# Conformer layer norm: variance sums laid out over token partitions, the inverse root spread back by TensorE

## Chip, cores and metric

One core of one Trainium2 chip runs the program once. The metric is the device time of that core in microseconds (us); lower is better. TensorE (PE) does matrix products, VectorE (DVE), ScalarE (ACT) and GpSimd (POOL) the rest, and SyncE (SP) issues the weight loads.

## The reference, cut to what matters

Two blocks run over a stream of 512 tokens by 1024 features. The change lies in the second block's second layer, in the convolution module and its layer norm:

```
def layernorm(x, g, b):
    mu = jnp.mean(x32, axis=-1, keepdims=True)
    var = jnp.mean(jnp.square(x32 - mu), axis=-1, keepdims=True)
    return ((x32 - mu) * lax.rsqrt(var + LN_EPS) * g + b).astype(x.dtype)

def conformer_conv(h, w_in, b_in, dw, dw_b, ln_g, ln_b, w_out, b_out):
    u = h @ w_in + b_in
    u = u[..., :D] * jax.nn.sigmoid(u[..., D:])
    u = causal_dwconv(u, dw) + dw_b
    u = jax.nn.silu(layernorm(u, ln_g, ln_b))
    return u @ w_out + b_out
```

After it comes a cross attention, whose keys and values `memn @ w_kv` depend on the memory alone and so can be computed at any time before.

## The kernel before

Everything is kept transposed: features on the 128 partitions, in KD = 8 tiles `m`, and the 512 tokens along the free dimension. A product runs as a `Linear` stage. One output tile of it is 8 x 3 matmuls (a float32 weight is split into a rounded part `w_hi` and a rest `w_lo`, and so is the input, L363 to L365), its weights are one chunk of 128 x 1024, and the split of each chunk is done two chunks ahead: ACT makes `w_hi` (L452), POOL `w_lo` (L460). Each engine's instructions stand in the order in which the Python methods of the stages write them; nothing is reordered, and every hand-over is a semaphore.

The three stages here are: the convolution's input product; `kv`, the 16 tiles of keys and values with 256 columns (`ms_hi`, `ms_lo`, outputs in PSUM banks 4 to 7); and `out`, the product with `w_out`, whose input tiles `ys_hi` and `ys_lo` are the normed, activated convolution. The layer norm has no stage of its own. It is written into the steps `t` = 0 to 15 of `kv`: `memory_tensor` is called after tile `t`'s matmuls on PE, and `memory_scalar` at the same step on ACT, behind the split of a chunk and behind `keys.taken`, which copies tile `t` out of PSUM (L2640) and so waits for its matmuls. `memory_vector` is one piece of DVE work.

The steps of the norm, with the names of the program: the mean by products with a matrix of ones (L2927); `gn_centred`, the mean taken off `conv_y` by DVE (L2955); `gn_squared`, the squares `ln_sq` by ACT (L2981, step 12); `gn_var`, the sum of the squares over features (`variance_tensor`, L2935); `gn_root` (L2984); `gn_inverse` (L2957); then for each `m` the product with gain and inverse root on DVE (L2965, `gn_scaled`), Silu on ACT (L2988), the rounded `ys_hi` on ACT (L2990) and the rest `ys_lo` on DVE (L2962, `fed`). PE's first tile of `out` takes the pairs `ys_hi`, `ys_lo` one `m` at a time as `fed` reports them, and every later tile of `out` follows without a wait.

Of the kernel before, what the change touches and what calls it, by code (L numbers as in the profile page):

```python
# [8 lines left out]
ACT = mybir.ActivationFunctionType  # L9
# [3 lines left out]
P = 128  # L13
T = 512
D = 1024
KD = D // P
# [51 lines left out]
class Signal:  # L68


    def __init__(self, nc, name):
        self.sem = nc.alloc_semaphore(name)
        self.base = 0
# [95 lines left out]
def as_float(t):  # L169

    return t.bitcast(F32)
# [1392 lines left out]
class Recurrence:  # L1564
# [184 lines left out]
    def spread_tensor(self, pe, p):  # L1749

        if p:
            self.wait(pe, "key_normed", p)
        else:
            self.wait(pe, "kk_inverse", 2)
        self.done(pe.matmul(self.k.ps[:, 6, :], self.spread[0:2 * KD, self.chunk(p)], self.rt[0:2 * KD, :], start=True,
                            stop=True), "spread")
# [1051 lines left out]
class Conformer:  # L2808
# [5 lines left out]
    def __init__(self, k, at, top, ready, prev):  # L2814
        self.k = k
        room = at(17)
        self.u, self.sg = at(0).tile("conv_u", KD, T + TAPS - 1), room.tile("conv_s", 2, T)
        self.rt, self.y, self.diag = room.tile("ln_rt", T), at(64).tile("conv_y", KD, T), at(80).tile("conv_dg", 4, PE_TAPS, P)
        self.sq = Arena(k, top).tile("ln_sq", KD, T)
        self.out = Halves(at(0).tile("ys_hi", KD, T, dtype=F32R), at(80).tile("ys_lo", KD, T, dtype=F32R))  # L2820
        self.used, self.free, self.sig_r, self.scaled = k.marks("chunk_used", "bank_free", "sigmoid_made", "normed_sums")
        self.dg, self.padz, self.summed, self.added, self.kept = k.marks("diagonals", "zeroed", "taps_summed", "taps_added",
                                                                         "conv_taken")
        self.norm = k.marks("gn_mean", "gn_centred", "gn_squared", "gn_var", "gn_root", "gn_inverse", "gn_scaled",
                            "gn_shifted", "fed_hi", "fed")
        self.handed = self.norm[9]
        self.linear = Linear(k, 2 * KD, KD, k.ahead, act=self.inputs_scalar, vector=self.inputs_vector, pool=self.inputs_pool,
                             fill=self.inputs_tensor, unroll=True, norm=True, bank=4, ready=ready, prev=prev)
        k.advance(KD, "sigmoid_made", "taps_summed", "conv_taken")
        k.advance(2 * KD, "normed_sums")  # L2830
        k.advance(KD * PE_TAPS, "diagonals")
        k.advance(1, "zeroed", "gn_mean", "gn_var", "gn_root", "gn_inverse")
        k.advance(KD * (TAPS - PE_TAPS), "taps_added")
        k.advance(KD, "gn_centred", "gn_squared", "gn_scaled", "gn_shifted", "fed_hi", "fed")
# [95 lines left out]

    def variance_tensor(self, pe, m):

        sq = self.norm[2]
        pe.wait_ge(sq.sem, sq(m + 1))
        mm = pe.matmul(self.k.ps[:, 1, :], self.k.ones[:, :], self.sq[:, m, :], start=(m == 0), stop=(m == KD - 1))  # L2935
        if m == KD - 1:
            mm.then_inc(self.norm[3].sem, 1)

    def memory_tensor(self, pe, t):
        if t == 0:  # L2940
            self.taps_tensor(pe, KD - 1)
        for m in {6: (0, 1, 2), 7: (3, 4, 5), 11: (6, 7)}.get(t, ()):
            self.mean_tensor(pe, m)
        for m in {13: (0, 1, 2, 3), 14: (4, 5, 6, 7)}.get(t, ()):
            self.variance_tensor(pe, m)

    def memory_vector(self, v, i, j):
        if i or j:
            return
        k, y = self.k, self.y  # L2950
        me, ce, sq, va, rt, iv, n1, n2, hi, fed = self.norm
        self.taps_vector(v, self.BOUNDS[KD], 4 * self.PAIR_OPS)
        v.wait_ge(me.sem, me(1))
        for m in range(KD):
            v.scalar_tensor_tensor(y[:, m, :], k.ps[:, 0, :], -1.0 / D, y[:, m, :], ALU.mult, ALU.add).then_inc(ce.sem, 1)  # L2955
        v.wait_ge(rt.sem, rt(1))
        v.reciprocal(k.ps[:, 2, :], self.rt[:, :]).then_inc(iv.sem, 1)  # L2957
        v.wait_ge(iv.sem, iv(1))

        def rest(m):  # L2960
            v.wait_ge(hi.sem, hi(m + 1))
            v.tensor_tensor(self.out.lo[:, m, :], y[:, m, :], as_float(self.out.hi[:, m, :]), ALU.subtract  # L2962
                            ).then_inc(fed.sem, 1)
        for m in range(KD):
            v.scalar_tensor_tensor(y[:, m, :], y[:, m, :], k.vec("cln_g", m), k.ps[:, 2, :], ALU.mult, ALU.mult  # L2965
                                   ).then_inc(n1.sem, 1)
            if m >= 2:
                rest(m - 2)
        rest(KD - 2)
        rest(KD - 1)  # L2970

    def memory_scalar(self, act, i, j):
        k, y, m = self.k, self.y, 4 * i + j
        me, ce, sq, va, rt, iv, n1, n2, hi, fed = self.norm
        self.keys.taken(act, 4, m)
        if m in (4, 10):
            self.keep(act, {4: 2, 10: 3}[m])
        if m == 12:
            for n in range(KD):
                act.wait_ge(ce.sem, ce(n + 1))  # L2980
                act.activation(self.sq[:, n, :], y[:, n, :], ACT.Square).then_inc(sq.sem, 1)  # L2981
        if m == 14:
            act.wait_ge(va.sem, va(1))
            act.activation(self.rt[:, :], k.ps[:, 1, :], ACT.Sqrt, scale=1.0 / D, bias=k.bias[1e-5]).then_inc(rt.sem, 1)  # L2984
        if m == 15:
            for n in range(KD):
                act.wait_ge(n1.sem, n1(n + 1))
                act.activation(y[:, n, :], y[:, n, :], ACT.Silu, bias=k.vec("cln_b", n)).then_inc(n2.sem, 1)  # L2988
                act.wait_ge(n2.sem, n2(n + 1))
                act.activation(self.out.hi[:, n, :], y[:, n, :], ACT.Copy).then_inc(hi.sem, 1)  # L2990


def conv_ffn(k, layer, at, tmp, ready, gain=None):
# [300 lines left out]
```

## Time and profile before

| | us |
|---|---|
| Time, median of 3 runs | 2587.29 (2586.89 to 2590.23) |
| The profiled execution: its time | 2576.17 |
| The profiled execution: its span | 2574.4 |
| PE busy over the span | 2484.3 |

The span runs from the first to the last instruction of the profile; 1.8 us of the profiled execution's time lie around it. The profiled execution was 11 us shorter than the median of the timed runs, so a change is worked out against its own time and then added to the median.

### The profile page before, as it was taken

What the parts mean: (1) busy time and instruction counts of PE and PEld (TensorE: products, weight loads), DVE (VectorE), ACT (ScalarE), POOL (GpSimd) and SP (SyncE); (2) the same over time, 40 slices, a digit from 0 to 9 for tenths busy, and PEclk for the clock granted to TensorE, in tenths of its full rate; (3) what the DMA queues carried; (4) which work ended last, traced back from release to release, by engine and by line L of the source; (5) the groups of instructions that cost most, each with busy time, mean ns of one, the idle gap of its engine ahead of it and who ended that gap; (6) DMA issues with size and microseconds to landing.
All of it is one profiled execution on the core that took longest, in us unless ns stands there. A gap on an engine that the chain in (4) does not pass through costs nothing.

```text
span 2574.4 us, 32184 instructions
## 1 busy us (share of the span) xinstructions
PE 2484.3 (96%) x12188; PEld 1927.1 (75%) x12188; DVE 1163.2 (45%) x1969; ACT 937.1 (36%) x1580; POOL 1021.0 (40%) x618
## 2 busy tenths in 40 slices
PE   7999999999989999999999999999999899999997
PEld 5776567888846668885787888888767787888886
DVE  5113744113052675734623364264399433562462
ACT  3544653222245462223433323123323534322222
POOL 4331545444522332212552544345324443444344
PEclk9999999999999999999999999999999999999998
DMA  3222012333311110002331233223222222233231
GB/s 123 65 66 87 18 34 90 99 97 93 124 49 52 56 58 2 2 1 93 116 106 46 92 94 112 77 94 100 80 66 90 91 82 66 86 95 114 82 98 66
DMA packets 54415, 196.98 MB, mean 77 GB/s; under 512 B 6573, under 2 KB 6701, under 8 KB 53581
## 3 DMA queue, kind: packets, MB, share of 16 engines
q1 hardware_dynamic: 53312, 192.44, 23.8%
q10 hardware_dynamic: 974, 2.80, 0.3%
q8 instruction: 84, 1.38, 0.2%
q14 instruction: 45, 0.37, 0.1%
HBM read 193.12 MB, written 2.10 MB: 76 GB/s over the span
## 4 chain that ended last, share of the span: by engine, by line
PE 45%; DVE 7%; ACT 1%; issue 0%; POOLq 0%; POOL 0%; DVEq 0%; ACTq 0%
PE ps L363 11%; PE ps L365 11%; PE ps L364 11%; DVE ps L2878 5%; PE ps L436 3%; PE ps L438 3%; PE ps L437 3%; PE ps L2721 1%; PE ps L2744 1%; PE ps L2891 1%; DVE ps L3040 0%; PE ps L2489 0%; PE ps L2521 0%; PE ps L2731 0%; PE ps L2935 0%
## 5 line engine op out<-in xcount | busy, mean ns | idle before, releaser
L460 POOL TENSOR_TENSOR w_lo<-raw,w_hi 128x1024 fp32r<-128x1024 f32 x342 | 819.3, 2406 | 1008.9 <-ACT w_hi L452 1008.8
L363 PE MATMUL ps<-ahead_hi,w_hi 128*128 128x512 f32 x1216 | 481.0, 396 | 2.0 <-issue 2.0
L365 PE MATMUL ps<-ahead_hi,w_lo 128*128 128x512 f32 x1216 | 473.3, 389 | 0.0
L364 PE MATMUL ps<-ahead_lo,w_hi 128*128 128x512 f32 x1216 | 473.1, 389 | 0.0
L452 ACT ACTIVATE w_hi<-raw 128x1024 fp32r<-128x1024 f32 x342 | 352.9, 1049 | 170.4 <-PE ps L438 91.1
L621 DVE TENSOR_TENSOR x_stream<-x_stream,ps 128x512 f32<-128x512 f32 x80 | 55.0, 687 | 474.5 <-PE ps L365 278.5
L363 PEld LDWEIGHTS ps<-ahead_hi,w_hi 128*128 128x128 f32 x1216 | 228.3, 188 | 52.9 <-issue 6.4
L364 PEld LDWEIGHTS ps<-ahead_lo,w_hi 128*128 128x128 f32 x1216 | 228.3, 188 | 50.9 <-issue 4.1
L365 PEld LDWEIGHTS ps<-ahead_hi,w_lo 128*128 128x128 f32 x1216 | 228.2, 188 | 48.0
L3012 ACT ACTIVATE ffn_s<-ps 128x512 f32<-128x512 f32 x44 | 26.3, 598 | 322.2 <-DVE ps L3040 322.2
L436 PE MATMUL ps<-ffn_a_hi,w_hi 128*128 128x512 f32 x352 | 137.4, 390 | 3.0 <-DVE ffn_a_lo L3045 2.9
L438 PE MATMUL ps<-ffn_a_hi,w_lo 128*128 128x512 f32 x352 | 137.0, 389 | 0.0
L437 PE MATMUL ps<-ffn_a_lo,w_hi 128*128 128x512 f32 x352 | 136.9, 389 | 0.0
L2878 DVE SCALAR_TENSOR_TENSOR ps<-conv_u,vecs,ps 128x512 f32<-128x512 f32 x192 | 127.1, 748 | 14.5 <-PE ps L2891 14.5
L654 POOL TENSOR_TENSOR squares<-squares,sqr 128x512 f32<-128x512 f32 x56 | 74.7, 1333 | 126.5 <-ACT sqr L645 70.8
L3023 DVE TENSOR_TENSOR ffn_u<-ps,root 128x512 f32<-128x512 f32 x88 | 60.6, 688 | 133.1 <-PE ps L365 133.0
L3040 DVE SCALAR_TENSOR_TENSOR ps<-ffn_u,vecs,ps 128x512 f32<-128x512 f32 x176 | 119.8, 749 | 0.0
L363 PE MATMUL ps<-hidden_hi,w_hi 128*128 128x512 f32 x256 | 99.6, 389 | 0.0
L364 PE MATMUL ps<-hidden_lo,w_hi 128*128 128x512 f32 x256 | 99.6, 389 | 0.0
L365 PE MATMUL ps<-hidden_hi,w_lo 128*128 128x512 f32 x256 | 99.6, 389 | 0.0
L363 PE MATMUL ps<-h_hi,w_hi 128*128 128x512 f32 x192 | 79.7, 415 | 17.1 <-DVE w_lo L245 13.3
L644 ACT ACTIVATE ahead_hi<-x_stream,vecs 128x512 fp32r<-128x512 f32 x48 | 34.8, 725 | 142.6 <-DVE x_stream L621 115.4
(419 smaller groups left out, 4579.4 us busy)
## 6 DMA issues: line engine op xcount, KB each, us to landing
raw<-in_wall SPq DMA_DIRECT2D x346, 512.0 KB, 3.6
x_stream<-in_x SPq DMA_DIRECT2D x8, 256.0 KB, 7.2
cw<-in_cmp_w SPq DMA_DIRECT2D x1, 2048.0 KB, 8.0
out_y<-x_stream SPq DMA_DIRECT2D x8, 256.0 KB, 2.1
lora_a<-in_lora_a ACTq DMA_DIRECT2D x1, 1152.0 KB
dist<-in_consts SPq DMA_DIRECT2D x1, 1088.0 KB, 11.1
mem<-in_mem SPq DMA_DIRECT2D x1, 1024.0 KB, 5.7
gwb<-in_lora_b SPq DMA_DIRECT2D x1, 1024.0 KB
```

Source lines behind the costliest of these rows:

```text
L363: pe.matmul(out, hi, src.hi[:, t, 0:width], start=first, stop=False)
L364: pe.matmul(out, hi, src.lo[:, t, 0:width], start=False, stop=False)
L365: return pe.matmul(out, lo, src.hi[:, t, 0:width], start=False, stop=last)
L436: pe.matmul(out, hi, src.hi[:, q, 0:width], start=(q == 0), stop=False)
L437: pe.matmul(out, hi, src.lo[:, q, 0:width], start=False, stop=False)
L438: mm = pe.matmul(out, lo, src.hi[:, q, 0:width], start=False, stop=(q == kt - 1))
L452: e.activation(self.w.hi[:, s, :], self.raw[:, s, :], ACT.Copy).then_inc(hi_r.sem, 1)
L460: e.tensor_tensor(self.w.lo[:, s, :], self.raw[:, s, :], as_float(self.w.hi[:, s, :]), ALU.subtract).then_inc(lo_r.sem, 1)
L654: e.tensor_tensor(k.squares[:, :], k.squares[:, :], sqt[:, m % 2, :], ALU.add).then_inc(ac.sem, 1)
L2878: v.scalar_tensor_tensor(bank, self.u[:, m, t:t + T], self.tap(m, t), bank, ALU.mult, ALU.add).then_inc(self.added.sem, 1)
L3023: e.tensor_tensor(ub[:, j, 2:T + 2], k.ps[:, 4 + j, :], k.root[:, :], ALU.mult).then_inc(ub_r.sem, 1)
L3040: e.scalar_tensor_tensor(bank, ub[:, m % 4, t:t + T], col, bank, ALU.mult, ALU.add).then_inc(cv.sem, 1)
```

## The change

The sum of squares over features is computed the other way round. Before, the 128 x 128 ones were the stationary operand and the squares of all 512 tokens the moving one, four feature tiles after `kv` tile 13 and four after tile 14; the sum of every token came out on all 128 partitions. Now the squares are the stationary operand, in four blocks of 128 tokens, and one column of ones moves: 32 matmuls whose output is one column each, all after tile 13. A token's sum then stands on one partition, and the sums fill a 128 x 4 tile. ACT takes the root of 128 x 4 numbers in step 13 instead of 128 x 512 in step 14; DVE inverts 128 x 4. `spread_tensor`, new, follows `kv` tile 14 on PE: four matmuls with the inverse roots of a block, broadcast along the free dimension, as stationary operand and the identity as moving one, which lay the inverse root of every token on all partitions of PSUM bank 2. DVE's scaling waits for this (`gn_spread`). On ACT, Silu and rounding of the first two feature tiles move from step 15 to step 14, ahead of a split and of the copy of tile 15.

```diff
     def variance_tensor(self, pe, m):
-        sq = self.norm[2]
+        ce, sq = self.norm[1:3]
+        if m == 0:
+            pe.wait_ge(ce.sem, ce(KD))
         pe.wait_ge(sq.sem, sq(m + 1))
-        mm = pe.matmul(self.k.ps[:, 1, :], self.k.ones[:, :], self.sq[:, m, :], start=(m == 0), stop=(m == KD - 1))
+        for b in range(4):
+            mm = pe.matmul(self.k.ps[:, b, 0:1], self.sq[:, m, b * P:(b + 1) * P], self.k.ones[:, 0:1], start=(m == 0),
+                           stop=(m == KD - 1))
         if m == KD - 1:
             mm.then_inc(self.norm[3].sem, 1)
+    def spread_tensor(self, pe):
+        iv = self.norm[5]
+        pe.wait_ge(iv.sem, iv(1))
+        for b in range(4):
+            mm = pe.matmul(self.k.ps[:, 2, b * P:(b + 1) * P], self.rt[:, 8 + b:9 + b].to_broadcast([P, P]), self.k.ident, start=True,
+                           stop=True)
+        mm.then_inc(self.spread.sem, 1)
     def memory_tensor(self, pe, t):
-        for m in {13: (0, 1, 2, 3), 14: (4, 5, 6, 7)}.get(t, ()):
-            self.variance_tensor(pe, m)
+        if t == 13:
+            for m in range(KD):
+                self.variance_tensor(pe, m)
+        if t == 14:
+            self.spread_tensor(pe)
     def memory_vector(self, v, i, j):
-        v.reciprocal(k.ps[:, 2, :], self.rt[:, :]).then_inc(iv.sem, 1)
-        v.wait_ge(iv.sem, iv(1))
+        v.reciprocal(self.rt[:, 8:12], self.rt[:, 0:4]).then_inc(iv.sem, 1)
+        v.wait_ge(self.spread.sem, self.spread(1))
     def memory_scalar(self, act, i, j):
-        if m == 14:
+        if m == 13:
             act.wait_ge(va.sem, va(1))
-            act.activation(self.rt[:, :], k.ps[:, 1, :], ACT.Sqrt, scale=1.0 / D, bias=k.bias[1e-5]).then_inc(rt.sem, 1)
-        if m == 15:
-            for n in range(KD):
+            act.activation(self.rt[:, 0:4], k.ps[:, 0:4, 0], ACT.Sqrt, scale=1.0 / D, bias=k.bias[1e-5]).then_inc(rt.sem, 1)
+        for n in {14: (0, 1), 15: range(2, KD)}.get(m, ()):
```

On PE, this is the place from the end of `kv` tile 13 to the end of tile 14, before the change (`ps<-ln_sq,ones` are the sums of squares, the other rows the matmuls of `kv`):

```order
L2935 MATMUL ps<-ln_sq_10656,ones 128x512 x4
L363 MATMUL ps<-ms_hi_10627,w_hi_10622 128x256
L364 MATMUL ps<-ms_lo_10628,w_hi_10622 128x256
L365 MATMUL ps<-ms_hi_10627,w_lo_10623 128x256
...
L2935 MATMUL ps<-ln_sq_10656,ones 128x512 x4
```

And the same place of the changed kernel:

```order
L2940 MATMUL ps<-ones,ln_sq_10656 128x1 x32
L363 MATMUL ps<-ms_hi_10627,w_hi_10622 128x256
L364 MATMUL ps<-ms_lo_10628,w_hi_10622 128x256
L365 MATMUL ps<-ms_hi_10627,w_lo_10623 128x256
...
L2950 MATMUL ps<-consts,ln_rt_10653 128x128 x4
```

All squares are summed ahead of tile 14 now, in 32 matmuls of one output column, and where the second half of the sums stood there are the four matmuls of the spread.

On ACT, this is the place from the squares (step 12) to the first rounded tiles (step 15), before the change (`ln_rt` is the root, `conv_y` the Silu in place, `kv_turned` the copy of a `kv` tile):

```order
L2981 ACTIVATE ln_sq_10656<-conv_y_10654 128x512 x8
L452 ACTIVATE w_hi_10622<-raw_10621 128x1024
L2640 ACTIVATE kv_turned_10631<-ps 128x256
L452 ACTIVATE w_hi_10622<-raw_10621 128x1024
L2640 ACTIVATE kv_turned_10631<-ps 128x256
L2984 ACT_TABLE_LOAD
L2984 ACTIVATE ln_rt_10653<-ps,eps 128x512
L452 ACTIVATE w_hi_10622<-raw_10621 128x1024
L2640 ACTIVATE kv_turned_10631<-ps 128x256
L2988 ACT_TABLE_LOAD
L2988 ACTIVATE conv_y_10654<-conv_y_10654,vecs 128x512
L2990 ACTIVATE ys_hi_10657<-conv_y_10654 128x512
```

And in the changed kernel, from the copy of tile 13 to the third Silu:

```order
L3002 ACT_TABLE_LOAD
L3002 ACTIVATE ln_rt_10653<-ps,eps 128x4
L452 ACTIVATE w_hi_10622<-raw_10621 128x1024
L2640 ACTIVATE kv_turned_10631<-ps 128x256
L3005 ACT_TABLE_LOAD
L3005 ACTIVATE conv_y_10654<-conv_y_10654,vecs 128x512
L3007 ACTIVATE ys_hi_10657<-conv_y_10654 128x512
L3005 ACTIVATE conv_y_10654<-conv_y_10654,vecs 128x512
L3007 ACTIVATE ys_hi_10657<-conv_y_10654 128x512
L452 ACTIVATE w_hi_10622<-raw_10621 128x1024
L2640 ACTIVATE kv_turned_10631<-ps 128x256
L3005 ACTIVATE conv_y_10654<-conv_y_10654,vecs 128x512
```

The root stands one split and one copy earlier, and two Silus with their roundings stand ahead of the last split and the last copy, which now lie between the second and the third Silu.

## Rows read from the trace of the kernel before

**Rows 1.** The page, part 1: busy us (share of the span), instructions

```profile
PE 2484.3 (96%) x12188; PEld 1927.1 (75%) x12188; DVE 1163.2 (45%) x1969; ACT 937.1 (36%) x1580; POOL 1021.0 (40%) x618
```

**Rows 2.** The chain that ended last, 1960 to 2060 us: start, us, what

```profile
2009.79 3.43 PE ps L2935 x8
...
2019.56 0.70 ACT ln_rt L2984
2020.29 3.37 DVE ps L2957
...
2035.56 0.50 PE ps L363
2036.06 0.23 PE ps L364
```

**Rows 3.** PE's timeline: start, us, engine, line, operation, idle before it and releaser

```profile
2009.63 3.59 PE L2935 MATMUL ps<-ln_sq,ones 128*128 128x512 f32 x8
2012.66 0.68 PE L363 MATMUL ps<-ms_hi,w_hi 128*128 128x256 f32 x1
...
2015.93 3.59 PE L2935 MATMUL ps<-ln_sq,ones 128*128 128x512 f32 x8
...
2026.72 0.77 PE L363 MATMUL ps<-ys_hi,w_hi 128*128 128x512 f32 x1 [4.33 <-DVE ys_lo L2962]
```

**Rows 4.** ACT's timeline, 2007 to 2028 us

```profile
2007.23 4.26 ACT L2981 ACTIVATE ln_sq<-conv_y 128x512 f32<-128x512 f32 x8
2011.39 1.04 ACT L452 ACTIVATE w_hi<-raw 128x1024 fp32r<-128x1024 f32 x1
2012.34 0.36 ACT L2640 ACTIVATE kv_turned<-ps 128x256 f32<-128x256 f32 x1
...
2016.13 0.38 ACT L2640 ACTIVATE kv_turned<-ps 128x256 f32<-128x256 f32 x1 [2.48 <-PE ps L365]
2016.53 1.28 ACT L2984 ACT_TABLE_LOAD   x1
...
2022.43 0.38 ACT L2640 ACTIVATE kv_turned<-ps 128x256 f32<-128x256 f32 x1 [1.23 <-PE ps L365]
2022.83 1.28 ACT L2988 ACT_TABLE_LOAD   x1
2024.46 0.72 ACT L2988 ACTIVATE conv_y<-conv_y,vecs 128x512 f32<-128x512 f32 x1 [0.35 <-DVE conv_y L2965]
...
2027.03 0.71 ACT L2988 ACTIVATE conv_y<-conv_y,vecs 128x512 f32<-128x512 f32 x1
```

**Rows 5.** PE's timeline, 39 to 42 us, in the first block's gates

```profile
39.66 1.85 PE L813 MATMUL ps<-gates_w,xg 128*128 128x12 f32 x16
41.37 0.48 PE L363 MATMUL ps<-h_hi,w_hi 128*128 128x512 f32 x1
```

**Rows 6.** DVE's timeline, 2001 to 2024 us

```profile
2004.09 4.88 DVE L2955 SCALAR_TENSOR_TENSOR conv_y<-ps,conv_y 128x512 f32<-128x512 f32 x8 [2.80 <-PE ps L2927]
```

**Rows 7.** Groups by line and shape: line, operation, shapes, count | busy, mean ns | idle before

```profile
L2756 DVE RECIPROCAL xst<-xst 128x1 f32<-128x1 f32 x32 | 5.1, 160 | 2.6 <-ACT xp L2773 2.1
```

**Rows 8.** PE's timeline: the same sixteen L2136 matmuls twice, and an L2106 group

```profile
999.49 3.68 PE L2136 MATMUL ps<-X,Tt 128*128 128x64 f32 x16
...
1028.80 2.00 PE L2136 MATMUL ps<-X,Tt 128*128 128x64 f32 x16
...
1105.36 1.14 PE L2106 MATMUL ps<-Tt,U 64*64 64x64 f32 x16
```

**Rows 9.** Windows: length, busy of PE, PEld, DVE, ACT, POOL, granted clock, DMA share, GB/s

```profile
998.00:1006.00 8.00, 8.00 (x52) 7.22 (x49) 0.46 (x2) 1.14 (x4) 2.48 (x5) 0.50 0.00 0
...
1106.50:1107.00 0.50, 0.50 (x3) 0.50 (x4) 0.00 (x0) 0.46 (x1) 0.00 (x0) 0.66 0.00 0
1107.00:1110.00 3.00, 3.00 (x22) 2.44 (x21) 0.00 (x0) 0.28 (x2) 0.00 (x0) 0.50 0.00 0
1110.00:1110.50 0.50, 0.50 (x6) 0.50 (x6) 0.00 (x0) 0.50 (x3) 0.00 (x0) 0.93 0.00 0
...
2024.50:2025.00 0.50, 0.00 (x0) 0.00 (x0) 0.50 (x1) 0.50 (x1) 0.00 (x0) 0.84 0.56 90
...
2031.50:2032.00 0.50, 0.50 (x3) 0.27 (x2) 0.50 (x2) 0.47 (x2) 0.00 (x0) 0.83 0.00 0
```

More of the change, by code:

```diff
@@ L2825, in __init__ @@
                             "gn_shifted", "fed_hi", "fed")
+        self.spread = k.marks("gn_spread")
+        k.advance(1, "gn_spread")
         self.handed = self.norm[9]
@@ L2981, in memory_scalar @@
                 act.activation(self.sq[:, n, :], y[:, n, :], ACT.Square).then_inc(sq.sem, 1)
-        if m == 14:
+        if m == 13:
             act.wait_ge(va.sem, va(1))
-            act.activation(self.rt[:, :], k.ps[:, 1, :], ACT.Sqrt, scale=1.0 / D, bias=k.bias[1e-5]).then_inc(rt.sem, 1)
-        if m == 15:
-            for n in range(KD):
[L2987 to L2990, printed above, removed]
+            act.activation(self.rt[:, 0:4], k.ps[:, 0:4, 0], ACT.Sqrt, scale=1.0 / D, bias=k.bias[1e-5]).then_inc(rt.sem, 1)
+        for n in {14: (0, 1), 15: range(2, KD)}.get(m, ()):
+            act.wait_ge(n1.sem, n1(n + 1))
+            act.activation(y[:, n, :], y[:, n, :], ACT.Silu, bias=k.vec("cln_b", n)).then_inc(n2.sem, 1)
+            act.wait_ge(n2.sem, n2(n + 1))
+            act.activation(self.out.hi[:, n, :], y[:, n, :], ACT.Copy).then_inc(hi.sem, 1)
 def conv_ffn(k, layer, at, tmp, ready, gain=None):
```

## Prediction

> **What bounds the kernel now.** I began with the page's busy times: PE is busy 2484.3 us, 96% of the span [rows 1], so only work that PE does, or a wait of PE, is worth time. Next I read the chain that ended last around the norm. Nearly everywhere it is PE; here it leaves PE. It goes through the last four of the variance matmuls, then the root on ACT (0.70 us), then the inverse on DVE (3.37 us), and comes back to PE at 2035.56 us with the last input tile of `out` [rows 2]. PE's timeline shows the hole: tile 15 of `kv` follows the second half of the sums, and then PE sits idle 4.33 us, until `ys_lo` releases it at 2026.72 [rows 3]. ACT's timeline shows what sets the pace from there. The first Silu starts at 2024.46, the third at 2027.03, so one feature tile takes 1.28 us (Silu and rounding together) [rows 4]. The eighth reaches PE at 2035.56 [rows 2], 8.53 us after the third Silu. PE needs less than that for a feature tile's three matmuls. From 2035.56 on PE runs without a wait. So the time of the kernel moves by exactly as much as this last feature tile moves, and that one hangs on the start of the Silus.
>
> **The change, term by term.** All starts come from rows; what runs before 2009.63 is untouched.
>
> *The sums on PE.* Removed: two groups of four matmuls, each 8 records in 3.43 us [rows 2], together 6.86 us. Added: 32 matmuls with 128 x 128 float32 weights and one moving column. A float32 matmul shows as two records, so 64. The nearest row is the gates' product: the same weights, 12 moving columns. Its 16 records take from 39.66 to 41.37, 0.107 us each [rows 5]; it is paced by the weight loads, which do not shrink with the columns. 64 x 0.107 = 6.84 us. The lower bound is a record that hides its weight load (priced as a rival); the upper is the clock, below. I take 0.107. So PE's total work is the same to 0.02 us, and only its place changes: all 6.84 us stand ahead of tile 14, none behind it. Sums end at 2009.63 + 6.84 = 2016.47. The wait for the squares costs nothing: eight squares take 4.26 us from 2007.23 [rows 4], 0.53 each, and PE takes 0.86 for each. The new wait for `gn_centred` is over when DVE's last subtraction ends, 2004.09 + 4.88 = 2008.97 [rows 6], 0.66 us before PE gets there.
>
> *Root and inverse.* Before, the root started about 0.2 us behind the last sum. Now it starts at about 2016.65 and has 4 numbers per partition instead of 512. The table load of 1.28 us is no obstacle: it can start behind the copy of tile 13 at 2012.34 [rows 4] and is over by 2014.2. The inverse of 128 x 512 took 3.37 us [rows 2]; the nearest small one takes 0.160 us [rows 7]. Both are over by 2017.1, while PE is in tile 14, so the 3.37 us leave the path.
>
> *The spread.* Tile 14 took from 2012.66 to 2015.93 [rows 3]; it moves by 6.84 - 3.43 = 3.41 us and ends at 2019.34. The four spread matmuls are 8 records at 0.107 (bounded by 0.125, the sixteen records in 2.00 us of [rows 8]): 0.86 to 1.0 us. With 0.2 us of hand-over DVE starts scaling at 2020.4 and the first Silu could start 0.78 later, at 2021.2.
>
> *ACT.* Its copy of tile 14 moves from 2016.13 [rows 4] to 2019.54. The Silu table load followed the copy by 0.40 us and took 1.28 [rows 4]: 2019.94 to 2021.22. So both paths meet and the first Silu starts at 2021.25 instead of 2024.46, 3.2 us earlier. But between the second and the third Silu there are now a split and the copy of tile 15, 0.95 + 0.26 = 1.21 us, by the distances of the same two instructions at 2011.39 and 2012.34 [rows 4]. Waiting behind them are Silus 3 to 8, and for those PE. Tile 15 has ended by then (2020.2 + 3.3 = 2023.5 against 2024.8), so this is no further wait. Third Silu: 2021.25 + 2.57 + 1.21 = 2025.03 against 2027.03. **Sum at full clock: -2.0 us.** The split delayed by this (chunk for `out` tile 1, needed by PE at about 2036) and the one delayed by the root in step 13 (chunk for tile 0) are POOL's next; both are made by 2027 (by 2031 with the fall below), before they are needed, and the weight loads of SP that hang on them have four chunks of lead.
>
> *The clock.* The sum above has a condition: for 6.84 us PE multiplies almost nothing, one column per weight load. The profile shows that the clock can fall although PE never stands still. At 1105.36 to 1106.43 PE runs 64-column matmuls [rows 8] and at 1106.66 (0.66 in the half microsecond from 1106.50) the granted clock goes to 0.50, the 1.2 GHz level, with PE busy in every row [rows 9]. From 998 to 1006 it stays there for the whole eight microseconds under 64- and 128-column matmuls [rows 9], and the sixteen L2136 records take 3.68 us in it instead of 2.00 [rows 8]. These matmuls carry 64 columns or more; ours carry one. So I expect the clock to fall inside the sums and to come back inside tile 14 or after it. All of the PE work in such a stretch is on the path (sums, tile 14, spread), and at half clock a stretch costs half its length. The stretches of this profile: 1106.66 to 1110.03, 3.4 us; 2024.84 to 2031.59 (worked out like the first from the rows with 0.84 and 0.83), about 6.8; and over 8 from 998 on, about 10 [rows 9]. Costs: 1.7, 3.4 and about 5. I take the middle one, since the low-activity work here goes on for some time after the fall, as there. Cost 3.4. Everything behind the sums moves with it, the Silu table load too. **Sum with the fall: -2.0 + 3.4 = +1.4 us**, between -0.3 and +3.0.
>
> The Trainium skill, "TensorE: Matmul & The Clock Gate", in the table under "Why this matters for your kernels", ties a falling clock to gaps in which TensorE is idle and advises issuing matmuls back to back. There is no gap here, so by that rule the change would give -2.0 us. The rows at 1106 speak against it: the clock fell with no gap.
>
> The Trainium skill, "ScalarE: Activation LUTs", section "What ACT_TABLE_LOAD costs", adds a drain of about 1.38 us to each load of 1.28 us. By that the first Silu would wait until about 2022.6 and the full-clock sum be -0.7 us. The load at 2022.83 had its Silu running 0.35 us after its end, and that gap was a wait for DVE, so the trace does not show the drain behind a load.
>
> **The rivals.** (1) *The clock stays up* (the page's rule as a mechanism): weight loads count as activity, or the sums end before the clock reacts. For it speaks that the gates' 12-column burst ran at full pace; but it lasted only 1.85 us [rows 5]. -2.0 us, 2585.3. Chance 0.13. (2) *A slower kernel*: the clock is still at half when the last feature tile enters PE. Up to then ACT's pace hides it, since three 512-column matmuls at half clock take about the 1.28 us that ACT takes. Behind it, nothing hides it, and each of the 24 matmuls of an `out` tile takes 0.46 instead of 0.23 us [rows 2], 5.5 us more per tile. With one whole tile that is 1.4 + 5.5 = +6.9, 2594.2. It decides from about 17 slow matmuls on (3.8 us lost). For it: the two gaps of PE behind the second feature tile, now some 1.8 us because of the split and copy. Against: a rise at about 2031.6 under just such fed-in matmuls [rows 9]. Chance 0.04. (3) *Weight loads hidden*: if one-column records cost a third, 2.3 us in all, tile 14 starts at about 2012 and the Sqrt table load (done 2014.2) and the copy set the Silus, first Silu about 2017.3; -7.2 + 1.2 = -6.0, 2581.3. [rows 5] speak clearly against it. Chance 0.03. The likeliest, the fall, has 0.80.
>
> **How the numbers follow.** Own time: 2576.17 + 1.4 = 2577.6 for a profiled execution; the median is 2587.29, which gives 2588.7. The three timed runs spread by 3.3 us, so I widen the cases' 2585.3 to 2590.3 by about 1.5 on each side: 2584 to 2592. A change of 0.2% is 5.2 us, about what a measurement of this kernel can tell from no change; both likely cases are well within it, whichever sign. Within: 0.90. Faster by more: rival 3 and a lucky clock, 0.05. Slower by more: rival 2, 0.05.
>
> **What would show it.** The 64 records at 0.107 us each in the beginning and 0.21 after a fall; granted clock 0.5 from some point between 2012 and 2016.5 until inside or just behind tile 14; inverse below 0.2 us; first Silu near 2021.3 without a fall and near 2024.6 with it; 3.8 us from the first to the third Silu instead of 2.57; last feature tile on PE at 2033.6 without and near 2037 with the fall. Wrong would be: a start-to-start well under 0.107, a full clock throughout, or a low clock in `out` tile 1.

## The result and the profile after

| | before | after |
|---|---|---|
| Median, 12 runs each, us | 2587.8 (2581.25 to 2591.73) | 2594.0 (2580.01 to 2595.68) |
| Ratio after to before | | 1.0018, 95% interval 1.0009 to 1.0026 |
| Span of the profiled execution, us | 2574.4 | 2593.4 |

By the ratio the change costs about 4.7 us, 0.18%, with an interval of 2.3 to 6.7 us; the two medians lie 6.2 us apart. The ratio's value is the forecast direction at more than three times the forecast size of 1.4 us, and the median lies above the range of 2584 to 2592. The two first profiles differ by 19 us, most of which has nothing to do with the change: the first sum of squares starts at 2009.63 us before [rows 3] and at 2023.72 after, so 14 us were there already (the last section comes back to it). The measure used from here on is therefore a *local time*: from PE's first sum to the start of the last input tile in `out` tile 0. Before it is 2035.56 - 2009.63 = 25.93 us [rows 2, 3].

PE's timeline of the changed kernel, with the rows that answer to [rows 3] and the last input tile:

```profile
2023.72 11.68 PE L2940 MATMUL ps<-ones,ln_sq 128*128 128x1 f32 x64
2035.26 0.56 PE L363 MATMUL ps<-ms_hi,w_hi 128*128 128x256 f32 x1
...
2040.09 1.05 PE L2950 MATMUL ps<-consts,ln_rt 128*128 128x128 f32 x8
...
2044.24 0.47 PE L363 MATMUL ps<-ys_hi,w_hi 128*128 128x512 f32 x1 [0.23 <-DVE ys_lo L2980]
2045.43 0.50 PE L363 MATMUL ps<-ys_hi,w_hi 128*128 128x512 f32 x1 [0.26 <-DVE ys_lo L2980]
2048.64 0.50 PE L363 MATMUL ps<-ys_hi,w_hi 128*128 128x512 f32 x1 [2.25 <-DVE ys_lo L2980]
...
2054.30 0.50 PE L363 MATMUL ps<-ys_hi,w_hi 128*128 128x512 f32 x1
```

The local time is 2054.30 - 2023.72 = 30.58 us, 4.65 us more than before. The 64 records of the sums take 11.54 us up to the start of tile 14, instead of 6.84. The old hole of 4.33 us is gone, and a new one of 2.25 us stands behind the second feature tile, where ACT makes a split and a copy.

Windows of the same execution (length, busy of the five engines, granted clock, DMA share, GB/s):

```profile
2023.70:2025.70 2.00, 2.00 (x21) 2.00 (x19) 0.00 (x0) 2.00 (x5) 0.00 (x0) 1.00 0.78 254
2026.00:2039.00 13.00, 13.00 (x62) 13.00 (x62) 0.18 (x1) 3.29 (x5) 4.63 (x2) 0.50 0.14 42
2039.50:2044.00 4.50, 4.50 (x38) 4.31 (x37) 2.66 (x4) 3.63 (x5) 0.00 (x0) 1.00 0.34 117
```

PE counts as busy in every microsecond, yet the granted clock is 0.50, the 1.2 GHz level, from 2.2 us behind the first sum until just before the spread. (Row by row in half microseconds the stretch adds up to 13.65 us.) Each of the thirteen profiles below has one more low stretch, in the first tile of `out`: 2024.84 to 2031.67 before, 2049.8 to 2053.2 in the changed kernel. It costs nothing there: from the start of the third Silu to the last input tile it is 8.53 to 8.55 us in all of them, so ACT's pace hides it.

ACT's and DVE's timelines show that the rest of the change does what it should:

```profile
2035.43 0.26 ACT L3002 ACTIVATE ln_rt<-ps,eps 128x4 f32<-128x4 f32 x1 [7.34 <-PE ps L2940]
...
2040.29 0.38 ACT L2640 ACTIVATE kv_turned<-ps 128x256 f32<-128x256 f32 x1 [3.65 <-PE ps L365]
2040.69 1.28 ACT L3005 ACT_TABLE_LOAD   x1
2041.98 0.72 ACT L3005 ACTIVATE conv_y<-conv_y,vecs 128x512 f32<-128x512 f32 x1
...
2045.77 0.71 ACT L3005 ACTIVATE conv_y<-conv_y,vecs 128x512 f32<-128x512 f32 x1
```

```profile
2035.73 0.18 DVE L2975 RECIPROCAL ln_rt<-ln_rt 128x4 f32<-128x4 f32 x1 [12.68 <-ACT ln_rt L3002]
```

The inverse takes 0.18 us instead of the 3.37 us of [rows 2]. The first Silu starts straight behind its table load; from it to the third Silu there are 3.79 us instead of the 2.57 us of [rows 4].

### The profile page after: what moved, and what is told of

Same layout as the page of the kernel before. It is cut to its first block, busy times and chain, and to the rows that moved or that the text cites. A ratio compares the mean times of both kernels' runs of the same rounds, so it can differ in the third digit from the quotient of the medians.

```text
span 2593.4 us, 32297 instructions
## 1 busy us (share of the span) xinstructions
PE 2507.9 (97%) x12244; PEld 1950.6 (75%) x12244; DVE 1160.8 (45%) x1969; ACT 936.9 (36%) x1580; POOL 1020.9 (39%) x618
## 4 chain that ended last, share of the span: by engine, by line
PE 46%; DVE 6%; ACT 1%; issue 0%; POOLq 0%; POOL 0%; DVEq 0%; ACTq 0%
PE ps L363 11%; PE ps L365 11%; PE ps L364 11%; DVE ps L2880 4%; PE ps L436 3%; PE ps L437 3%; PE ps L438 3%; PE ps L2721 1%; PE ps L2744 1%; PE ps L2893 1%; PE ps L2940 0%; DVE ps L3057 0%; PE ps L2489 0%; PE ps L2521 0%; PE ps L2731 0%
## 5 line engine op out<-in xcount | busy, mean ns | idle before, releaser
L363 PE MATMUL ps<-ahead_hi,w_hi 128*128 128x512 f32 x1216 | 482.0, 396 | 2.0 <-issue 2.0
L363 PEld LDWEIGHTS ps<-ahead_hi,w_hi 128*128 128x128 f32 x1216 | 228.7, 188 | 53.2 <-issue 6.4
L363 PE MATMUL ps<-hidden_hi,w_hi 128*128 128x512 f32 x256 | 99.6, 389 | 0.0
L363 PE MATMUL ps<-h_hi,w_hi 128*128 128x512 f32 x192 | 79.6, 414 | 17.2 <-DVE w_lo L245 13.7
```

Of the source, the lines that this page charges most:

```text
L363: pe.matmul(out, hi, src.hi[:, t, 0:width], start=first, stop=False)
```

## Experiments

**The theories.** Theory 1: the whole loss is TensorE's clock. One-column matmuls occupy PE but give it next to nothing to multiply; the clock goes to its lower level inside the sums, and that low stretch lies on the path. Without it the change would gain about 2 us. Rival: the clock is a side show, and the loss comes from the order of ACT (split and copy between the Silus) or from 32 small matmuls and their hand-overs.

All local times, worked out from the same two rows of each profile. wide, wide15, order15, halves and twice are edits of the changed kernel; whole13, early and early2 are edits of the kernel before; after_b and before_b are the two kernels unedited. after_b, before_b, twice, wide15, halves and halves_b were executed once each, so only their local times are used:

| kernel | first sum | last input tile | local us | clock in sums and `kv` tiles |
|---|---|---|---|---|
| before | 2009.63 | 2035.56 | 25.93 | 1.00 |
| before_b | 2022.72 | 2048.65 | 25.93 | 1.00 |
| after | 2023.72 | 2054.30 | 30.58 | 0.50 for 13.65 us |
| after_b | 2022.73 | 2053.33 | 30.60 | 0.50 for 13.65 us |
| wide | 2022.09 | 2046.31 | 24.22 | 1.00 |
| wide15 | 2013.41 | 2040.17 | 26.76 | 1.00 |
| order15 | 2021.87 | 2051.80 | 29.93 | 0.50 for 6.83 us |
| halves | 2009.89 | 2038.79 | 28.90 | 0.50 twice, 6.83 us together |
| halves_b | 2024.05 | 2056.07 | 32.02 | 0.50 twice, 13.66 us together |
| twice | 2021.31 | 2065.55 | 44.24 | 0.50 from 2 us on |
| whole13 | 2008.59 | 2032.86 | 24.27 | 1.00 |
| early | 2024.27 | 2048.21 | 23.94 | 1.00 |
| early2 | 2024.00 | 2047.33 | 23.33 | 1.00 |

**wide: more columns behind the same weight loads.**

```diff
-            mm = pe.matmul(self.k.ps[:, b, 0:1], self.sq[:, m, b * P:(b + 1) * P], self.k.ones[:, 0:1], start=(m == 0),
+            mm = pe.matmul(self.k.ps[:, b, 0:P], self.sq[:, m, b * P:(b + 1) * P], self.k.ones[:, :], start=(m == 0),
```

> One edit of the changed kernel: 128 columns of ones move past each block of squares instead of one, so the same 32 weight loads and products issue in the same order, and only PE's arithmetic per load is larger. Local measure: from the first sum matmul to the last input tile of out on PE, 25.9 us before (2009.63 to 2035.56), 30.6 us after the change (2023.72 to 2054.30). Theory 1 (the clock fell because one-column matmuls are next to no work, and all of the loss is the low stretch over the sums and tile 14): the granted clock stays 1.00 through sums and tile 14, the sums take 64 x 0.107 to 0.125 = 6.8 to 8.0 us instead of 11.5, local 23.9 to 25.0, time about 2 us under before. Rival (the loss is the order of ACT, or the loads and hand-overs of 32 small matmuls): local stays near 30.6 and the time near that of the changed kernel.

PE's timeline and windows of wide:

```profile
2022.09 7.31 PE L2940 MATMUL ps<-ones,ln_sq 128*128 128x128 f32 x64
2029.16 0.36 PE L363 MATMUL ps<-ms_hi,w_hi 128*128 128x256 f32 x1
...
2032.10 1.05 PE L2950 MATMUL ps<-consts,ln_rt 128*128 128x128 f32 x8
...
2046.31 0.50 PE L363 MATMUL ps<-ys_hi,w_hi 128*128 128x512 f32 x1
```

```profile
2022.09:2029.10 7.01, 7.01 (x65) 7.01 (x64) 0.00 (x0) 4.36 (x7) 2.35 (x1) 1.00 0.29 91
2029.10:2037.00 7.90, 7.67 (x62) 7.20 (x60) 3.82 (x7) 5.82 (x9) 2.39 (x1) 1.00 0.37 119
```

128 times the columns, and the sums take less time: 64 records in 7.07 us, 0.110 each, against 11.54 us. The clock stays at 1.00. Local 24.22 us, 6.4 us under the changed kernel and 1.7 under before. Theory 1 holds, and the rival is out as the cause of the loss: the order of ACT, the number of matmuls and their hand-overs are the same in these two kernels. The time was 2586.99 us, the ratio to before 0.9974 (0.9957 to 0.9991); 0.26% is 6.7 us, more than the 1.7 us that the local time accounts for. The likely reason is told in the last section: five of its eleven runs lay at 2572 to 2577 us, with a mean granted clock of 0.987 to 0.989 against 0.981 in the others. Its median is only 0.9 us below that of the kernel before (2587.89 us). So the whole time fits a gain but does not measure it; the 1.7 us rest on the local time.

**after_b and before_b: the two kernels once more.**

> The changed kernel once more, for a second look at where the clock falls. Theory 1: it falls inside the sums again, 2 to 6 us behind the first, and stays down into tile 14; local is 24.2 us (what wide measured at full clock) plus half of the low stretch, so 27.5 to 31. Rival (the fall in the first profile was chance): clock 1.00 there and local 24.2.

> The kernel before once more: clock 1.00 from the first sum to the end of tile 15 and local 25.9 us, whatever the time of the whole kernel does.

Both local times repeat to 0.02 us. Here the first sum starts at the same time in both (2022.73 and 2022.72), and the spans of 2592.4 and 2586.8 us differ by much less than the first pair: 5.6 us, of which 4.7 are local and 0.9 lie behind the last input tile.

**twice: the dose doubled.** The accumulation over feature tiles is left out, so its root is of other numbers.

```diff
-        for b in range(4):
+        for b in (0, 1, 2, 3, 0, 1, 2, 3):
             mm = pe.matmul(self.k.ps[:, b, 0:1], self.sq[:, m, b * P:(b + 1) * P], self.k.ones[:, 0:1], ...
```

> The changed kernel with each of the 32 one-column matmuls issued twice, so 128 records instead of 64 (accumulation over feature tiles is left out, each sum holds the last tile only). Theory 1: the clock falls early in them and cannot come back before they end, so the 64 more cost 0.213 us each: 13.6 us more, local 41 to 45 us, low stretch above 20 us. Rival (a low stretch has its length whatever runs in it, the clock then returns): the added ones cost 0.107 each, local about 6.8 us above the changed kernel's.

PE's timeline and a window of twice:

```profile
2021.31 25.26 PE L2940 MATMUL ps<-ones,ln_sq 128*128 128x1 f32 x128
...
2065.55 0.47 PE L363 MATMUL ps<-ys_hi,w_hi 128*128 128x512 f32 x1
```

```profile
2024.00:2046.00 22.00, 22.00 (x104) 22.00 (x105) 0.00 (x0) 1.67 (x3) 2.35 (x1) 0.50 0.07 25
```

Local 44.24 us, 13.7 more than the changed kernel; 64 x 0.213 = 13.6. Once down, the clock did not come back while these matmuls went on. It is one profile, but far from the 6.8 us that a low stretch of fixed length would have added.

**halves: the one-column sums back in two places.**

```diff
-        if t == 13:
-            for m in range(KD):
-                self.variance_tensor(pe, m)
-        if t == 14:
+        for m in {13: (0, 1, 2, 3), 14: (4, 5, 6, 7)}.get(t, ()):
+            self.variance_tensor(pe, m)
+        if t == 15:
             self.spread_tensor(pe)
```

Not shown: the root moves to step 14 and all Silus to step 15.

> The one-column sums in the places of the old ones, four feature tiles behind tile 13 and four behind tile 14, root in step 14, spread behind tile 15, all Silus in step 15. Theory 1 in the form that a full 6.8 us of one-column work in one piece is what brings the clock down: two pieces of 3.4 us with a tile of 2.9 us between may leave it at 1.00; then sums 3.4 us each, first Silu 14.5 us behind the first sum, local about 25.6. If each piece alone is enough, the clock is at 0.50 in one of them or in a tile, and local is 27 to 29.

> The same kernel as halves again, since where the clock moves differs from run to run: 25.6 with the clock at 1.00, 27 to 29 with a fall.

PE's first piece in halves and the tile behind it, then windows in that tile and in the one behind the second piece:

```profile
2009.89 3.63 PE L2940 MATMUL ps<-ones,ln_sq 128*128 128x1 f32 x32
2013.38 0.36 PE L363 MATMUL ps<-ms_hi,w_hi 128*128 128x256 f32 x1
```

```profile
2015.50:2018.00 2.50, 2.50 (x15) 2.50 (x13) 0.00 (x0) 0.31 (x1) 1.99 (x1) 0.50 0.58 182
2022.50:2024.50 2.00, 2.00 (x11) 2.00 (x11) 0.00 (x0) 0.23 (x1) 1.69 (x1) 0.50 0.00 0
```

And in halves_b, from inside each piece into the tile behind it:

```profile
2027.00:2032.00 5.00, 5.00 (x24) 5.00 (x25) 0.00 (x0) 1.06 (x2) 4.62 (x2) 0.50 0.31 84
2037.00:2043.00 6.00, 6.00 (x29) 6.00 (x30) 0.18 (x1) 1.21 (x2) 2.38 (x1) 0.50 0.05 8
```

My hope that a tile of 2.9 us between two pieces would hold the clock was wrong in both profiles. The clock fell once for each piece of 16 matmuls: in halves_b inside the pieces (at 2026.2 and 2036.5), in halves only behind them, in the full-size matmuls of the next tile (at 2014.6 and 2021.7). 25.6 us were expected without a fall; 28.90 and 32.02 came. The second lies above my 27 to 29 as well: again I took the stretches too short.

**order15 and wide15: the reordering on ACT.** order15 is the changed kernel with this edit, wide15 is wide with it.

```diff
-        for n in {14: (0, 1), 15: range(2, KD)}.get(m, ()):
+        for n in {15: range(KD)}.get(m, ()):
```

> The changed kernel with all eight Silus in step 15, behind the copy of tile 15. With the sums as slow as in the changed kernel's profile: the Silu table load waits for tile 15, first Silu some 3.9 us later, but no split and copy between second and third (1.2 us), so local 30.6 + 2.6 = 33.2 us. Rival (the order of ACT causes the loss): local falls to 26 to 29.

> wide (128 columns moving, clock kept) with all eight Silus in step 15, to price the reordering on ACT at full clock. Tile 15 ends about 3.9 us behind tile 14, so the copy, the Silu table load and the first Silu come 3.9 us less about 0.1 later than in wide, and no split and copy (1.2 us) stand between second and third: local 24.2 + 2.6 = 26.8 us. If the reordering is worth nothing, 24.2.

PE's timelines, first of order15, then of wide15:

```profile
2021.87 9.04 PE L2940 MATMUL ps<-ones,ln_sq 128*128 128x1 f32 x64
2030.78 0.56 PE L363 MATMUL ps<-ms_hi,w_hi 128*128 128x256 f32 x1
...
2051.80 0.50 PE L363 MATMUL ps<-ys_hi,w_hi 128*128 128x512 f32 x1 [0.31 <-DVE ys_lo L2980]
```

```profile
2013.41 7.31 PE L2940 MATMUL ps<-ones,ln_sq 128*128 128x128 f32 x64
...
2040.17 0.50 PE L363 MATMUL ps<-ys_hi,w_hi 128*128 128x512 f32 x1 [0.31 <-DVE ys_lo L2980]
```

wide15 settles it at full clock: 26.76 us, 2.54 above wide, where 2.6 was worked out. So two Silus in step 14 gain 2.5 us. And 26.76 is 0.83 above the kernel before: without them the earlier sums and the small inverse gain nothing. In the kernel before the Silu table load ends at 2022.83 + 1.28 = 2024.11, only 0.35 us ahead of the first Silu [rows 4], so the inverse held the first Silu back by no more than that as long as all Silus stood in step 15. order15 came out at 29.93, not 33.2, because my expectation took the low stretch of the first profile as given; here the clock fell only 5.1 us behind the first sum, the sums took 8.91 us instead of 11.54, and the stretch was 6.83 us. By its own clock it fits: wide15's 26.76 plus half of 6.83 is 30.2. Its time was 2595.23 us, ratio 1.0024 (1.0011 to 1.0038). It also shows that the low stretch over the same sums can differ in length: here it was 6.83 us, in both profiles of the changed kernel 13.65. What sets the moment of the fall, 2.2 us behind the first sum in after, after_b, twice and halves_b and about 5 in order15 and halves, stays open.

**whole13, early, early2: is the small inverse needed?** All three are edits of the kernel before. whole13 takes before's sums (ones stationary, 512 columns moving) and its wide inverse, and only moves them: all sums behind tile 13, root in step 13, two Silus in step 14, no spread.

```diff
-        for m in {13: (0, 1, 2, 3), 14: (4, 5, 6, 7)}.get(t, ()):
-            self.variance_tensor(pe, m)
+        if t == 13:
+            for m in range(KD):
+                self.variance_tensor(pe, m)
-        if m == 14:
+        if m == 13:
             act.wait_ge(va.sem, va(1))
-        if m == 15:
-            for n in range(KD):
+        for n in {14: (0, 1), 15: range(2, KD)}.get(m, ()):
```

> The sums as before the change (ones stationary, 512 columns moving), but all eight behind tile 13; root of 128 x 512 in step 13, the inverse of 128 x 512 on DVE as before, no spread; two Silus in step 14 as in the change. Theory 1: clock stays 1.00 in sums and tile 14, sums 6.86 us, root 0.7, inverse 3.4 us now beside tiles 14 and 15, first Silu 12.0 us behind the first sum, plus 3.8 to the third, local 24.2 us, that is 1.7 under before: the move of the sums gives the gain, and the small inverse and the spread add 0.3 us at most. Rival (the gain needs the 0.2 us inverse): local 25.9 or more.

DVE's timeline and ACT's first Silu in whole13:

```profile
2016.38 3.36 DVE L2958 RECIPROCAL ps<-ln_rt 128x512 f32<-128x512 f32 x1 [8.46 <-ACT ln_rt L2985]
```

```profile
2018.92 1.28 ACT L2988 ACT_TABLE_LOAD   x1
2020.55 0.72 ACT L2988 ACTIVATE conv_y<-conv_y,vecs 128x512 f32<-128x512 f32 x1 [0.34 <-DVE conv_y L2966]
```

The wide inverse costs 0.34 us of waiting here, as it runs beside the `kv` tiles and the table load. Local 24.27 us against wide's 24.22, which has the small inverse and the spread: the new layout is worth 0.05 us once the sums are moved. The time, 2588.14 us, ratio 0.9998 (0.999 to 1.0007), cannot show 1.7 us. early and early2 then make the last chunk's split ahead of the first Silu. early calls it in step 14 behind the copy of tile 14; early2 makes it in the `Linear` stage, ahead of that copy. The edit of early2:

```diff
                 if not (peel and ...) and (i, j) != getattr(self, "early", None):
                     self.split_step(i, j, step)
+                if (i, j + 1) == getattr(self, "early", None):
+                    self.split_step(i, j + 1, step)
...
+        self.kv.early = (3, 3)
```

> As whole13, and the split of the last chunk, which stood between the second and the third Silu, is made in step 14 ahead of the first Silu, where ACT waits for tile 14. Theory 1 with the ACT term of the sum: the distance from first to third Silu falls from 3.8 to 2.9 us, local 23.3 us, 2.6 under before. Rival (the split is not on the path): local as whole13.

> As early, with the last chunk's split made in front of the copy of tile 14, where ACT really waits (in early it stood behind that copy and pushed the first Silu from 11.96 to 12.58 us behind the first sum). Expected: first Silu at 12.0, third at 14.8, local 23.3 us against 25.93 before and 24.27 in whole13. If the split of a chunk cannot be made there without a wait, local as in early, 23.9.

In early, behind the copy, ACT was no longer idle, and the split pushed the first Silu back from 11.96 to 12.58 us behind the first sum: 23.94 us, not 23.3. ACT's timeline of early2:

```profile
2031.65 2.00 ACT L452 ACTIVATE w_hi<-raw 128x1024 fp32r<-128x1024 f32 x2
2033.93 0.38 ACT L2642 ACTIVATE kv_turned<-ps 128x256 f32<-128x256 f32 x1 [0.29 <-PE ps L365]
2034.34 1.28 ACT L2992 ACT_TABLE_LOAD   x1
2035.97 0.72 ACT L2992 ACTIVATE conv_y<-conv_y,vecs 128x512 f32<-128x512 f32 x1 [0.35 <-DVE conv_y L2970]
```

Both splits fit before the copy, the first Silu is 11.97 us behind the first sum (2024.00), and local is 23.33 us, 2.6 under before, the shortest here. Times: early 2587.15 us, ratio 1.0001 (0.999 to 1.0012); early2 2587.38 us, ratio 0.9994 (0.9985 to 1.0003). That early2 beats the kernel before is shown in the local time of one profile, not in the time of the whole.

## Why the prediction was wrong

- **What bounds the place**: right. The time moved with the last input tile: 4.65 us in the local time, 4.7 by the ratio. That they agree so closely is partly chance, as the ratio's interval is 2.3 to 6.7 us.
- **Sums at full clock, 0.107 us a record, 6.84 us**: not seen in the changed kernel; the nearest is wide, 7.07 us with 128 columns. In halves the first piece ran at full clock throughout, 32 records in 3.49 us up to the next tile, 0.109 each, so the term holds for one column as long as the clock does.
- **Root, inverse, spread**: right (0.26 and 0.18 us, spread 0.81 us up to tile 15 with the clock back up). The spread never had to wait for the inverse.
- **ACT**: right. Table load straight into the first Silu, 3.79 us to the third against 3.78 worked out. The drain that the Trainium skill adds to a table load ("ScalarE: Activation LUTs", "What ACT_TABLE_LOAD costs") does not show in this trace: the load starts 0.02 us after the copy ends, and the first Silu 0.01 us after the load ends.
- **Sum at full clock, -2.0 us**: wide gave -1.71, with sums of 7.07 us instead of 6.84.
- **That the clock falls, though PE never stands still**: right, and the rule of the Trainium skill that was weighed against it ("TensorE: Matmul & The Clock Gate", "Why this matters for your kernels", which names idle gaps) would have given -2.0 us. In these traces the clock fell in stretches without a gap.
- **The step that failed**: "I take the middle one", a low stretch of 6.8 us for 3.4 us of cost. It was 13.65 us. The excess over wide is 6.36 us instead of 3.4: 4.47 in the sums (11.54 against 7.07) and 1.89 in tile 14 (4.83 against 2.94). With wide's -1.71 that makes the +4.65. I had listed stretches of 3.4, 6.8 and 10 us as the bounds and thought the longest, 3.0 us in total, the worst. But those lengths came from other work, and this work lengthens itself: once the clock is down, the rest of the sums takes twice as long. In the eight stretches of after, after_b, order15, twice, halves and halves_b the clock came back 3.0 to 5.6 us behind the last one-column matmul before it, whether the whole stretch was 3.4 or 27.3 us long. Had the clock fallen 2.1 us into the sums, they alone were 2.1 + 44 x 0.213 = 11.5 us, which the rows at hand would have given; a range that reached to such an early fall would have held the result.
- **Where luck came in**: 6.8 us was not impossible. order15 has the same sums and a stretch of 6.83 us, and lies 3.2 us above wide15, close to the 3.4 of the forecast. The forecast direction, slower, hung on the same number: with wide's -1.71 us, a low stretch shorter than about 3.4 us would by my estimate have left a gain.
- **Two smaller errors that changed nothing**: the granted clock of 0.93 and 0.83 in the last half microseconds [rows 9] puts the ends of the two shorter stretches at 1110.07 and 2031.67, not 1110.03 and 2031.59; their lengths stay 3.4 and 6.8 us. The two gaps of PE behind the second feature tile, taken as 1.8 us, measured 2.25 and 0.30.

## To carry to other kernels

In these traces a record of a product with 128 x 128 float32 weights took 0.107 to 0.110 us at full clock whether 1, 12 or 128 columns moved. A run of such products with one column also lost the clock, for itself and for the full-size matmuls behind it; with 128 columns it did not. Where more columns cost no time, move many. When the fall of a clock is a term of the sum, price the case in which it falls at the start and the low-work run goes on at half speed, not a stretch length seen elsewhere. And before a new layout is built to shorten an operation, look whether moving the old one a step earlier already hides it: here that, with the two Silus, gave 1.66 of the 1.71 us, and wide15 shows that the two Silus were what it hung on.

## What the runs showed of the hardware

The two profiles of the same kernel, before and before_b, took 2576.17 and 2588.5 us with the same local time. Windows of the first, then of before_b, in the second block's first layer and behind it:

```profile
1150.00:1180.00 30.00, 29.70 (x280) 25.51 (x279) 11.54 (x36) 9.24 (x22) 5.02 (x8) 1.00 0.01 2
1195.00:1215.00 20.00, 17.98 (x48) 4.59 (x47) 5.83 (x9) 11.26 (x20) 7.92 (x9) 1.00 0.63 245
```

```profile
1155.00:1180.00 25.00, 25.00 (x183) 21.34 (x182) 5.19 (x15) 6.71 (x15) 4.92 (x8) 0.73 0.01 2
1195.00:1220.00 25.00, 21.96 (x102) 10.80 (x100) 7.57 (x20) 5.48 (x13) 0.69 (x1) 0.80 0.38 148
```

The same code ran once at full clock and once with some 13.7 and 10.2 us at the lower level (twice what the mean of a window lacks to 1.00, times its 25 us, gives 13.5 and 10). Both low stretches begin among many matmuls of 64 and 128 columns. A third place lies in the first block, windows of before and before_b:

```profile
280.00:290.00 10.00, 9.79 (x56) 6.61 (x56) 6.62 (x20) 3.14 (x13) 8.99 (x12) 1.00 0.19 54
```

```profile
280.00:290.00 10.00, 9.70 (x35) 6.96 (x35) 4.12 (x14) 1.31 (x7) 9.11 (x12) 0.66 0.17 54
```

What they cost can be read from matmuls that both profiles have. One L1139 matmul stands at 252.02 and 252.18 us, a group of the same line behind the third place at 286.18 and 289.40, an L2286 matmul at 1156.02 and 1159.55, and an L363 matmul behind all three at 1219.39 and 1232.50. So before_b loses 3.1 us in the third place and 9.6 in the two later ones, 0.3 in between; the spans differ by 12.4 us. Edited kernels have the same two kinds of execution (whole13's profiled one took 2572.79 us, most of its runs 2586 to 2589). This moves a time by some 12 us, more than twice what this change does, and it is why a local measure was needed. What decides which kind an execution becomes stays open; no run here looked for it.
